# Turning the first two heads of a linear attention inside the last projection block, with gating, rounding and remainders in a new order

## The chip, the core and the metric

The kernel runs on one core of a Trainium2 chip. The metric is the device time of one execution in microseconds (us): 650.53 us, the median of three runs from 649.70 to 651.06. One more execution was profiled; it took 651.25 us, and its span, from the first to the last instruction, is 649.5 us.

## What is computed

A trunk of two residual layers over 256 tokens of width 1024. Layer 0 mixes tokens by gated linear attention (GLA), layer 1 by block softmax attention; a squared-ReLU MLP follows each. The change lies in the GLA mixer of layer 0:

```python
q, k, v, r, glr = jnp.split(h @ w_in, splits, axis=-1)
...
o = (o_intra + o_inter).reshape(B, S, H, DV)          # 4 heads of 256 columns
o = rms_norm(o, onorm_g).reshape(B, S, H * DV) * jax.nn.silu(r.astype(f32))
return o.astype(h.dtype) @ w_out
```

Each sub-layer is modulated with shift, scale and gate from `mod = silu(c) @ ada_w[i] + ada_b[i]`, a product over 6 x 1024 columns a layer.

## The kernel before, in words

The program is written out by hand for each engine. The order on an engine is the order of its instructions; engines meet at semaphores (`wait_ge`, `then_inc`).

Weights come from HBM through SyncE's queue (SP) into `w_raw`, 1 MB (two *units* of 128 x 1024) per copy, with four slots of 1 MB. ScalarE (ACT) rounds each unit to `w_hi` (`hi`, L1051), VectorE (DVE) makes the remainder `w_lo` (`lo`, L1433), and TensorE (PE) multiplies three times per product: hi by hi, lo by hi, hi by lo (`three`, L503 to L505). `w_hi` and `w_lo` hold four units each, so `hi(u)` waits until PE has used unit u-4. `lo(u)` of the second unit of a pair frees a slot of `w_raw`.

The GLA mixer has eight blocks of four units. Blocks 0 to 5 project k, q, v and r; (n, u) is unit u of block n. Blocks 6 and 7 are the output projection. PE accumulates a block of 0 to 5 in two PSUM banks: 4 and 5 for even n, 6 and 7 for odd n. ACT and DVE work one block ahead of PE's numbering: their step (6, u) rounds unit u of block 6 while PE is in block 5. Tables `tasks` say what else an engine does after each step.

Behind the recurrence, for two pairs of heads (0 and 1):

- ACT takes squares and roots (`o_squares`, `o_root`), DVE forms the scales (`o_scales`) and `normed(pair)`, two rows of heads per token tile out of PSUM (L1690, four instructions).
- ACT reads r's block out of PSUM through SiLU (`read_in(0, 4)`, `read_in(0, 5)`, L1163, two instructions each). It first loads the SiLU/sine table (`silu_set`, L1209); `sines` serves layer 1.
- DVE multiplies (`gated(pair)`, L1702, two instructions). It waits for `in_out`, ACT's reads, and for `on_ok`, its own `normed`.
- PE turns the result (`turn_o(pair)`, L660, eight 128 x 128 transposes) into banks 4 and 5 (pair 0) or 6 and 7 (pair 1). It waits for `ot_ok`, the gated pair.
- ACT rounds each turned head (`o_hi`, L1158) to `a_hi` and DVE makes `a_lo` (`o_low`, L1587). Head q is used by unit q of block 6, which waits for `a_ok`.

Before the change, PE runs `turn_o(0)` behind block 5, then two products `fin_gate` for the gates (L622), which wait for `on_ok` 2, then block 6, with `turn_o(1)` behind its first unit and `sum_mods(1, 4)` (L583) behind its fourth. DVE's loop ends with `lo(6, 3)`, then `o_low` of heads 0 and 1, `gated(1)`, two `gate` (L1486), `o_low` of heads 2 and 3, and two `ada()`. Block 7 follows, with `turn_mods` (L591) on PE and `mods` (L1472) on DVE, then the residual, its norm `xn` (L1509) and PE's turn of `xn` (L631), which opens the MLP.

The modulation product for later sub-layers is made by DVE in pieces. `ada()` number s (from 0) takes 1 MB of `ada_w` from one of two buffers `ada_raw` in two instructions (L1450; the first of a group of four is L1447) and counts `ada_mac` up by 2. The copies are issued by GpSimd (POOL, L381), in order:

```python
for s in range(2, 4 * N_PAIRS_ADA):
    pool.wait_ge(ada_mac, 2 * (s - 1))
    load(s)
```

So copy s starts once `ada()` s-2 is done. `sum_mods` begins with `pe.wait_ge(ada_mac, 8 * (ada_turn(b0 + 3) + 1))`; for `sum_mods(1, 4)` that is 24, which is the end of `ada()` number 11. Of the twelve, one stands ahead of the loop, eight at the steps listed in `adas`, one in the task (5, 3), and two behind the loop.

Of the kernel before, what the change touches and what calls it, by code (L numbers as in the profile page):

```python
# [29 lines left out]
ACT = mybir.ActivationFunctionType  # L30
# [3 lines left out]
TB = 2  # L34
COLS = 512
# [12 lines left out]
def trunk_kernel(nc, x_d, c_d, pos_d, ada_w, ada_b, mix_g, mlp_g, gla_in, gla_up, gla_bg, gla_og,  # L48
                 gla_out, moba_in, moba_qg, moba_kg, moba_out, w1_d, w2_d, eye_d, keep_d, amask_d,
                 restart_d, invf_d, out_d):  # L50
    DEPTH, D = mix_g.shape
# [29 lines left out]
    with ctx:  # L81
# [67 lines left out]
        silu_r = area(2 * K1, TB, D)  # L149
# [144 lines left out]
        def in_bank(n, tb):  # L294
            return 4 + 2 * (n % 2) + tb
# [203 lines left out]
        def _(pe):  # L499
# [153 lines left out]
            def turn_o(pair):  # L653

                pe.wait_ge(in_out, 10 + 2 * pair)
                pe.wait_ge(ot_ok, pair + 1)
                for h in (2 * pair, 2 * pair + 1):
                    for k in (2 * h, 2 * h + 1):
                        for tb in range(TB):
                            z = tr(ps[:, 4 + h, (k % 2) * SEQ + tb * P:(k % 2) * SEQ + (tb + 1) * P],  # L660
                                   o_tok[:, tb, k * P:(k + 1) * P], eye[:, :])
                    z.then_inc(oT_ok, 1)
# [106 lines left out]
            def gla():  # L769
# [86 lines left out]
                def first_blocks(sides):  # L856

                    for s, (n, u) in enumerate(FIRST):
# [13 lines left out]
                        if (s, 2) in sides:  # L872
# [3 lines left out]
                         {0: turn_k, 1: turn_q, 3: turn_tail},  # L876
                         {0: scores, 2: lambda: update(0), 3: lambda: update(1)},
                         {0: lambda: update(2), 1: lambda: update(3), 2: lambda: output(0), 3: lambda: output(1)},
                         {}]
                pe.wait_ge(mod_red, 2)  # L880
                first_blocks({(0, 2): lambda: second_rows(2), (1, 2): lambda: (second_cols(2), second_rows(3)),
                              (2, 0): lambda: second_cols(3), (5, 2): glr, (6, 2): logits})
                for n in range(2, 6):
                    pe.wait_ge(in_out, 2 * (n - 1))
                    project(mix_base[0] + 4 * n, (in_bank(n, 0), in_bank(n, 1)), None, sides[n])
                turn_o(0)
                pe.wait_ge(on_ok, 2)
                for i in range(2):
                    fin_gate(4 + i, 2 + i)
# [133 lines left out]
        def _(act):  # L1023
# [3 lines left out]
            def link(ins):  # L1027

                steps[0] += 1
                ins.then_inc(act_step, 1)  # L1030
                act.wait_ge(act_step, steps[0])
# [21 lines left out]
            def hi_at(u):  # L1053
                hi(u, u % 8, u // 8)
# [105 lines left out]
            def read_in(l, n, dst, func=ACT.Copy):  # L1160
                act.wait_ge(unit_used, FIRST_DONE[n] if l == 0 and n < 2 else mix_base[l] + 4 * n + 4)
                for tb in range(TB):
                    A(dst[tb], ps[:, in_bank(n, tb), :], func).then_inc(in_out, 1)  # L1163

            def gla():
                def glr():
                    act.wait_ge(glr_p, 1)
                    A(glrT[:, :], ps[:, 0, 0:SEQ], ACT.Copy).then_inc(glr_ok, 1)

                def softplus():  # L1170

                    act.wait_ge(z_p, 1)
                    for h in range(GH):
                        if h == 2:
                            act.wait_ge(z_ok, 2)
                        A(g_t[:, h], ps[:, h // 2, (h % 2) * SEQ:(h % 2 + 1) * SEQ], ACT.Abs,
                          bias=cols[:, C_BG + h:C_BG + h + 1]).then_inc(za_ok, 1)
                    act.wait_ge(za_ok, GH)
                    link(A(g_t, g_t, ACT.Exp, scale=-1.0))
                    A(g_t, g_t, ACT.Ln, bias=1.0).then_inc(ez_ok, 1)  # L1180

                def decays():
                    act.wait_ge(G_ok, 1)
                    A(g_i, g_s, ACT.Exp, scale=-1.0 / 16).then_inc(eG_ok, 1)
                    A(g_t, g_t, ACT.Exp, scale=1.0 / 16).then_inc(eG_ok, 1)
                    A(g_e, g_s, ACT.Exp, scale=1.0 / 16).then_inc(eG_ok, 1)

                def tail():
                    act.wait_ge(kt_p, 1)
                    for tb in range(TB):  # L1190
                        z = A(k_tail[:, tb], ps[:, 2 + tb, :].rearrange("p (h d) -> p h d", h=GH), ACT.Copy)
                    z.then_inc(kt_ok, 1)

                def o_squares(pair):
                    act.wait_ge(o_p, pair + 1)
                    for tb in range(TB):
                        for h in (2 * pair, 2 * pair + 1):
                            j = S_O + 4 * tb + h
                            A(o_tok[:, tb, h * DV:(h + 1) * DV],
                              ps[:, 2 * pair + tb, (h % 2) * DV:(h % 2 + 1) * DV],  # L1200
                              ACT.Square, accum_out=stat[:, j:j + 1]).then_inc(oss_ok, 1)

                def o_root():
                    act.wait_ge(oss_ok, 8)
                    link(A(stat[:, S_O + 8:S_O + 16], stat[:, S_O:S_O + 8], ACT.Ln, scale=1.0 / DV, bias=eps[:, :]))
                    A(stat[:, S_O + 16:S_O + 24], stat[:, S_O + 8:S_O + 16], ACT.Exp, scale=-0.5).then_inc(or0_ok, 1)

                def silu_set():
                    nc.scalar.preload_act_table_set(SETS_SILU_SIN)  # L1209

                def sines():
                    act.wait_ge(sc_arg, 1)
                    A(trig[:, :, :], trig[:, :, :], ACT.Sin).then_inc(sc_ok, 1)

                def ln_exp_set():
                    nc.scalar.preload_act_table_set(SETS_LN_EXP)

                def k_in():
                    glr()
                    read_in(0, 0, [g_tok[:, 0, tb] for tb in range(TB)])  # L1220


                tasks = {
                    (2, 0): [k_in],
                    (2, 2): [softplus],
                    (2, 3): [lambda: read_in(0, 1, [g_tok[:, 1, tb] for tb in range(TB)]), decays],
                    (3, 2): [tail],
                    (3, 3): [lambda: read_in(0, 2, [g_v[:, tb, 0:COLS] for tb in range(TB)])],
                    (4, 3): [lambda: read_in(0, 3, [g_v[:, tb, COLS:D] for tb in range(TB)])],
                    (5, 2): [lambda: o_squares(0)],  # L1230
                    (5, 3): [lambda: o_squares(1), o_root],
                    (6, 0): [silu_set, sines,
                             lambda: read_in(0, 4, [silu_r[:, tb, 0:COLS] for tb in range(TB)], ACT.Silu)],
                    (6, 2): [lambda: read_in(0, 5, [silu_r[:, tb, COLS:D] for tb in range(TB)], ACT.Silu)],
                }
                for n in range(2, 7):
                    for u in range(4):
                        hi_at(mix_base[0] + 4 * n + u)
                        for t in tasks.get((n, u), []):
                            t()  # L1240
                for q in range(4):
                    o_hi(0, q)
                ln_exp_set()

# [166 lines left out]
        def _(dve):  # L1411
# [178 lines left out]
            def o_low(l, qs=range(4)):  # L1590
                for q in qs:
                    a_low(A_OUT[l] + q, q, ps[:, 4 + q, :].rearrange("p (c t) -> p c t", c=2), slice(0, SEQ))
# [22 lines left out]
            def gla():  # L1615
# [69 lines left out]
                def normed(pair):  # L1685

                    r = stat[:, S_O + 40:S_O + 48]
                    for tb in range(TB):
                        for h in (2 * pair, 2 * pair + 1):
                            z = V.scalar_tensor_tensor(o_tok[:, tb, h * DV:(h + 1) * DV],  # L1690
                                                       ps[:, 2 * pair + tb, (h % 2) * DV:(h % 2 + 1) * DV],
                                                       r[:, 4 * tb + h:4 * tb + h + 1], onorm[:, :],
                                                       op0=ALU.mult, op1=ALU.mult)
                    z.then_inc(on_ok, 1)

                def gated(pair):

                    cs = slice(pair * COLS, (pair + 1) * COLS)
                    dve.wait_ge(in_out, 10 + 2 * pair)
                    dve.wait_ge(on_ok, pair + 1)  # L1700
                    for tb in range(TB):
                        z = V.tensor_tensor(o_tok[:, tb, cs], o_tok[:, tb, cs], silu_r[:, tb, cs], ALU.mult)  # L1702
                    z.then_inc(ot_ok, 1)
# [3 lines left out]
                    (3, 3): [masked], (4, 1): [lambda: states(0)], (4, 2): [lambda: states(1)],  # L1707
                    (5, 0): [lambda: states(2)], (5, 1): [lambda: states(3)],
                    (5, 3): [ada, o_scales, lambda: normed(0)],
                    (6, 0): [lambda: normed(1), lambda: gated(0)],  # L1710
                }

                ada()
                adas = [(2, 0), (3, 1), (3, 2), (4, 0), (4, 2), (5, 0), (5, 2), (6, 1)]
                for n in range(2, 7):
                    for u in range(4):
                        lo_at(mix_base[0] + 4 * n + u)
# [1 line left out]
                            t()  # L1719
                        if (n, u) in adas:  # L1720
                            ada()
                o_low(0, range(2))
                gated(1)
                for i in range(2):
                    gate(i, 2 + i)
                o_low(0, range(2, 4))
                for _ in range(2):
                    ada()

# [248 lines left out]
```

## Time and profile before

| | |
|---|---|
| median of three runs | 650.53 us (649.70 to 651.06) |
| profiled execution | 651.25 us, span 649.5 us, mean granted TensorE clock 0.983 |
| PE busy | 621.5 us, 96% of the span |
| DVE busy | 474.5 us, 73% |
| ACT busy | 341.0 us, 53% |
| the stretch of the change | about 114 to 154 us from the span's start |

All times below are counted from the span's start. A line of a timeline gives start, length, engine, line, operation, what is written from what, and how many merged instructions; the brackets give the engine's idle time before it and what ended it. The lengths of neighbouring instructions overlap (a matmul of 512 columns is listed with 0.39 us, but the next one starts 0.23 us later), so steps are counted from start to start.

### The profile page before, as it was taken

How to read it: one execution, taken by the hardware profiler on the slowest of the kernel's cores; microseconds unless marked ns; L12 is line 12 of the kernel's file. 1: busy time of each engine (PE TensorE's matmuls, PEld its weight loads, DVE VectorE, ACT ScalarE, POOL GpSimd, SP SyncE). 2: the span in 40 equal slices, each digit the busy share in tenths (PEclk: the TensorE clock that was granted, in tenths of full speed). 3: DMA queues.
4: the chain of work that ended last, by engine and by line, in shares of the span. 5: the costliest groups of instructions: out<-in, count | busy, mean ns of one | idle time of the engine just before them, and what ended most of it. 6: DMA issues, size and time to landing. Idle time of an engine off the chain costs nothing.

```text
span 649.5 us, 9093 instructions
## 1 busy us (share of the span) xinstructions
PE 621.5 (96%) x3391; PEld 516.6 (80%) x3391; DVE 474.5 (73%) x660; ACT 341.0 (53%) x581; POOL 39.4 (6%) x65
## 2 busy tenths in 40 slices
PE   4699999899999999999999989999999999999997
PEld 2467875677889988998977767788788899899885
DVE  4638998889768978888986777956886555555455
ACT  3437632658645344534458657666854543454440
POOL 3030021000000110111100000000000000000000
PEclk9599999999999999999999989999999999999999
DMA  8999499667588998999964644533476555555501
GB/s 287 387 359 391 164 329 381 219 250 257 190 279 322 373 364 306 360 347 355 364 240 160 208 152 147 178 112 121 157 245 225 186 187 193 194 194 194 192 1 65
DMA packets 59084, 156.43 MB, mean 241 GB/s; under 512 B 2818, under 2 KB 3312, under 8 KB 59056
## 3 DMA queue, kind: packets, MB, share of 16 engines
q1 hardware_dynamic: 47296, 112.41, 49.2%
q0 software_dynamic: 11760, 43.67, 18.9%
q8 instruction: 15, 0.25, 0.2%
q14 instruction: 13, 0.11, 0.0%
HBM read 155.02 MB, written 1.05 MB: 240 GB/s over the span
## 4 chain that ended last, share of the span: by engine, by line
PE 78%; DVE 12%; ACT 4%; issue 3%; DMA 2%; SPq 0%; DVEq 0%; ACTq 0%
PE ps L503 13%; PE ps L504 13%; PE ps L505 13%; PE ps L700 7%; PE ps L699 7%; PE ps L698 7%; PE ps L510 3%; PE ps L512 3%; PE ps L511 3%; DVE w_lo L1433 2%; DMA arena<-in_ada_w_dram 2%; DVE spare L1433 1%; PE ps L607 1%; DVE ada_acc L1450 1%; PE ps L615 1%
## 5 line engine op out<-in xcount | busy, mean ns | idle before, releaser
L1051 ACT ACTIVATE w_hi<-w_raw 128x1024 fp32r<-128x1024 f32 x180 | 189.1, 1058 | 215.4 <-PE ps L505 117.7
L1433 DVE TENSOR_TENSOR w_lo<-w_raw,w_hi 128x1024 fp32r<-128x1024 f32 x180 | 218.3, 1222 | 109.5 <-ACT w_hi L1051 109.3
L700 PE MATMUL ps<-a_hi,w_lo 128*128 128x256 f32 x384 | 108.7, 283 | 0.0
L699 PE MATMUL ps<-a_lo,w_hi 128*128 128x256 f32 x384 | 108.7, 283 | 0.0
L698 PE MATMUL ps<-a_hi,w_hi 128*128 128x256 f32 x384 | 108.6, 283 | 0.0
L503 PE MATMUL ps<-w_hi,m_hi 128*128 128x512 f32 x256 | 100.4, 392 | 0.0
L504 PE MATMUL ps<-w_lo,m_hi 128*128 128x512 f32 x256 | 99.8, 390 | 0.0
L505 PE MATMUL ps<-w_hi,m_lo 128*128 128x512 f32 x256 | 99.7, 389 | 0.0
L503 PE MATMUL ps<-w_hi,a_hi 128*128 128x512 f32 x224 | 93.0, 415 | 5.1 <-DVE a_lo L1587 5.1
L504 PE MATMUL ps<-w_lo,a_hi 128*128 128x512 f32 x224 | 88.6, 396 | 0.0
L505 PE MATMUL ps<-w_hi,a_lo 128*128 128x512 f32 x224 | 88.6, 396 | 0.0
L1450 DVE SCALAR_TENSOR_TENSOR ada_acc<-ada_raw,c_act,ada_acc 128x1024 f32<-128x1024 f32 x56 | 71.7, 1281 | 3.3 <-DMA ada_raw<-in_ada_w_dram 1.9
L699 PEld LDWEIGHTS ps<-a_lo,w_hi 128*128 128x128 f32 x384 | 73.7, 192 | 0.5
L698 PEld LDWEIGHTS ps<-a_hi,w_hi 128*128 128x128 f32 x384 | 73.7, 192 | 0.5
L700 PEld LDWEIGHTS ps<-a_hi,w_lo 128*128 128x128 f32 x384 | 73.7, 192 | 0.0
L503 PEld LDWEIGHTS ps<-w_hi,a_hi 128*128 128x128 f32 x224 | 42.9, 191 | 19.3 <-issue 7.4
L503 PEld LDWEIGHTS ps<-w_hi,m_hi 128*128 128x128 f32 x256 | 48.1, 188 | 11.1 <-DVE w_lo L1433 0.8
L505 PEld LDWEIGHTS ps<-w_hi,m_lo 128*128 128x128 f32 x256 | 48.1, 188 | 10.1
L504 PEld LDWEIGHTS ps<-w_lo,m_hi 128*128 128x128 f32 x256 | 48.1, 188 | 9.3
L381 POOL DMA_DIRECT2D ada_raw<-in_ada_w_dram x40 | 28.2, 704 | 412.7 <-DVE ada_acc L1450 368.7
L505 PEld LDWEIGHTS ps<-w_hi,a_lo 128*128 128x128 f32 x224 | 42.8, 191 | 9.4
L504 PEld LDWEIGHTS ps<-w_lo,a_hi 128*128 128x128 f32 x224 | 42.9, 191 | 8.1
(202 smaller groups left out, 712.6 us busy)
## 6 DMA issues: line engine op xcount, KB each, us to landing
w_raw<-in_mlp_w_dram SPq DMA_DIRECT2D x64, 1024.0 KB, 5.6
ada_raw<-in_ada_w_dram POOLq DMA_DIRECT2D x40, 1024.0 KB, 7.0
w_raw<-in_gla_w_in_dram SPq DMA_DIRECT2D x12, 1024.0 KB, 13.4
w_raw<-in_moba_w_in_dram SPq DMA_DIRECT2D x12, 1024.0 KB, 7.1
ada_raw<-in_ada_w_dram SPq DMA_DIRECT2D x4, 1024.0 KB, 13.0
arena<-in_ada_w_dram SPq DMA_DIRECT2D x4, 1024.0 KB, 14.2
w_raw<-in_gla_w_out_dram SPq DMA_DIRECT2D x4, 1024.0 KB, 9.0
w_raw<-in_moba_w_out_dram SPq DMA_DIRECT2D x4, 1024.0 KB, 4.8
```

The costliest lines, as they stand in the source:

```text
L381: nc.gpsimd.dma_start(ada_pair(s), src.rearrange("(k p) n -> p k n", p=P)).then_inc(ada_sw_in[s % 2], 16)
L503: mm(out, hi, w_hi[:, slot, wc], start=first, stop=False)
L504: mm(out, hi, w_lo[:, slot, wc], start=False, stop=False)
L505: return mm(out, lo, w_hi[:, slot, wc], start=False, stop=last)
L510: mm(out, hi, unit_hi(u)[:, wc], start=first, stop=False)
L511: mm(out, hi, unit_lo(u)[:, wc], start=False, stop=False)
L698: mm(o, w_hi[:, u, w], a_hi[:, a, :], start=u == 0 and k == 0, stop=False)
L699: mm(o, w_hi[:, u, w], a_lo[:, a, :], start=False, stop=False)
L700: z = mm(o, w_lo[:, u, w], a_hi[:, a, :], start=False, stop=u == 3 and k == 1)
L1051: A(dst, w_raw[:, c // 2, c % 2], ACT.Copy).then_inc(hi_made, 1)
L1433: V.tensor_tensor(out, w_raw[:, c // 2, c % 2], w.bitcast(F32), ALU.subtract).then_inc(lo_made, 1)
L1450: z = V.scalar_tensor_tensor(acc, w, c, acc, op0=ALU.mult, op1=ALU.add)
```

## The change

PE: `turn_o(0)` moves from behind block 5 to behind its third unit. ACT, step (6, 0): the SiLU read goes ahead of `sines`. Step (6, 2): `o_hi` of heads 0 and 1 goes ahead of the second SiLU read; only heads 2 and 3 stay behind the loop. DVE, step (6, 0): `gated(0)` goes ahead of `normed(1)`. Step (6, 1): `o_low` of heads 0 and 1 and `gated(1)` come in, `ada()` number 9 goes out. Step (6, 3): `ada()` number 9, then `o_low` of heads 2 and 3. The two `gate` and the last two `ada()` stay behind the loop.

```diff
-                         {}]
+                         {2: lambda: turn_o(0)}]
...
-                turn_o(0)
                 pe.wait_ge(on_ok, 2)
...
-                    (6, 0): [silu_set, sines,
-                             lambda: read_in(0, 4, [silu_r[:, tb, 0:COLS] for tb in range(TB)], ACT.Silu)],
-                    (6, 2): [lambda: read_in(0, 5, [silu_r[:, tb, COLS:D] for tb in range(TB)], ACT.Silu)],
+                    (6, 0): [silu_set,
+                             lambda: read_in(0, 4, [silu_r[:, tb, 0:COLS] for tb in range(TB)], ACT.Silu), sines],
+                    (6, 2): [lambda: o_hi(0, 0), lambda: o_hi(0, 1),
+                             lambda: read_in(0, 5, [silu_r[:, tb, COLS:D] for tb in range(TB)], ACT.Silu)],
...
-                for q in range(4):
+                for q in (2, 3):
                     o_hi(0, q)
...
-                    (6, 0): [lambda: normed(1), lambda: gated(0)],
+                    (6, 0): [lambda: gated(0), lambda: normed(1)],
+                    (6, 1): [lambda: o_low(0, range(2)), lambda: gated(1)],
+                    (6, 3): [ada, lambda: o_low(0, range(2, 4))],
...
-                adas = [(2, 0), (3, 1), (3, 2), (4, 0), (4, 2), (5, 0), (5, 2), (6, 1)]
+                adas = [(2, 0), (3, 1), (3, 2), (4, 0), (4, 2), (5, 0), (5, 2)]
...
-                o_low(0, range(2))
-                gated(1)
                 for i in range(2):
                     gate(i, 2 + i)
-                o_low(0, range(2, 4))
```

## Rows read from the trace of the kernel before

**Rows 1.** The page's chain that ended last: share of the span by engine.

```profile
PE 78%; DVE 12%; ACT 4%; issue 3%; DMA 2%; SPq 0%; DVEq 0%; ACTq 0%
```

**Rows 2.** Waits, 100 to 165 us: total, times, longest.

```profile
PE ps L503 <- DVE a_lo L1587: 1.8, 1, 1.8
```

**Rows 3.** Timeline of PE, blocks 5 and 6.

```profile
122.74 0.39 PE L503 MATMUL ps<-w_hi,a_hi 128*128 128x512 f32 x1
...
125.46 1.03 PE L660 MATMUL ps<-eye,arena 128*128 128x128 f32 x8
126.33 1.88 PE L622 MATMUL ps<-ada_acc,ones 128*128 128x512 f32 x4
129.98 0.47 PE L503 MATMUL ps<-w_hi,a_hi 128*128 128x512 f32 x1 [1.77 <-DVE a_lo L1587]
...
132.83 1.03 PE L660 MATMUL ps<-eye,arena 128*128 128x128 f32 x8
...
136.45 0.39 PE L503 MATMUL ps<-w_hi,a_hi 128*128 128x512 f32 x1
...
141.98 1.06 PE L583 MATMUL ps<-ada_acc,ones 128*32 128x512 f32 x8
```

**Rows 4.** Timeline of ACT, steps (6, 0) to (6, 3).

```profile
118.63 1.28 ACT L1209 ACT_TABLE_LOAD   x1
...
120.25 1.07 ACT L1163 ACTIVATE arena<-ps 128x512 f32<-128x512 f32 x2
...
123.00 1.06 ACT L1051 ACTIVATE w_hi<-w_raw 128x1024 fp32r<-128x1024 f32 x1 [0.73 <-PE ps L505]
125.66 1.09 ACT L1163 ACTIVATE arena<-ps 128x512 f32<-128x512 f32 x2 [1.60 <-PE ps L505]
...
127.58 1.09 ACT L1158 ACTIVATE a_hi<-ps 128x512 fp32r<-128x512 f32 x2
```

**Rows 5.** Timeline of DVE from step (6, 0) to the modulation of the MLP.

```profile
120.46 1.65 DVE L1690 SCALAR_TENSOR_TENSOR arena<-ps,stat,onorm 128x256 f32<-128x256 f32 x4
122.03 1.28 DVE L1702 TENSOR_TENSOR arena<-arena 128x512 f32<-128x512 f32 x2
...
124.36 2.60 DVE L1450 SCALAR_TENSOR_TENSOR ada_acc<-ada_raw,c_act,ada_acc 128x1024 f32<-128x1024 f32 x2
...
129.15 1.28 DVE L1587 TENSOR_TENSOR a_lo<-ps,a_hi 128x512 fp32r<-128x512 f32 x2
...
131.55 1.28 DVE L1486 TENSOR_TENSOR gates<-ps,gates 128x512 f32<-128x512 f32 x2
...
135.30 5.30 DVE L1450 SCALAR_TENSOR_TENSOR ada_acc<-ada_raw,c_act,ada_acc 128x1024 f32<-128x1024 f32 x4
140.52 4.63 DVE L1433 TENSOR_TENSOR w_lo<-w_raw,w_hi 128x1024 fp32r<-128x1024 f32 x4
146.48 0.17 DVE L1472 TENSOR_TENSOR modc<-ps,cols 128x16 f32<-128x16 f32 x1 [1.33 <-PE ps L591]
```

**Rows 6.** Timeline of PE at the turn of `xn`.

```profile
153.53 1.07 PE L631 MATMUL ps<-eye,arena 128*128 128x128 f32 x8 [0.27 <-DVE arena L1509]
```

**Rows 7.** Timeline of POOL: the issue of copy 11.

```profile
127.26 0.70 POOL L381 DMA_DIRECT2D ada_raw<-in_ada_w_dram  x1 [12.05 <-DVE ada_acc L1450]
```

**Rows 8.** L381, issues at 127 to 128, 138 to 139, 170 to 260 us.

```profile
DMA to landing us min/median/max: 5.5/5.5/5.5
...
DMA to landing us min/median/max: 5.8/5.8/5.8
...
DMA to landing us min/median/max: 5.4/6.8/8.9
```

**Rows 9.** Timeline of PE at its longest wait for DVE after 100 us.

```profile
375.99 1.97 PE L906 MATMUL ps<-eye,arena 128*128 128x128 f32 x8 [3.33 <-DVE arena L1764]
```

**Rows 10.** Windows: length, five engines' busy time, granted clock, DMA share, GB/s.

```profile
128.00:129.00 1.00, 0.21 (x1) 0.00 (x0) 1.00 (x2) 0.66 (x2) 0.00 (x0) 1.00 1.17 389
...
376.00:377.00 1.00, 1.00 (x5) 1.00 (x6) 1.00 (x2) 0.08 (x1) 0.00 (x0) 0.50 0.00 0
```

## The prediction, made before the changed kernel ran

> **What bounds the kernel now.** I read the chain that ended last first: 78% of it is PE, 12% DVE, 4% ACT [rows 1]. Time can be won only where PE stands still or where a hand-over from DVE or ACT paces it. Next the waits of the stretch of the change: PE waits once for a remainder, 1.8 us [rows 2]. Then the timelines of the single engines, in which the reader is to see how that gap is made. PE turns pair 0 at 125.46, starts the gate products at 126.33 and the first unit of block 6 only at 129.98, after 1.77 us of idleness ended by `a_lo` [rows 3]. ACT rounds the turned heads from 127.58 because `hi(6, 3)` and the SiLU read stand ahead of it [rows 4]; DVE makes `a_lo` from 129.15, behind `ada()` number 9 (124.36, 2.60 us) and two `lo` [rows 5]. Last I read what waits behind block 6: `sum_mods` starts at 141.98, as soon as block 6 is through, and it may, since `ada()` number 11 ended at 135.30 + 5.30 = 140.60 [rows 3, 5]. Its cover is 1.4 us. That is the point where I expect the gain to be handed back.
>
> **PE up to block 6.** The third unit of block 5 ends where the fourth starts, at 122.74; a unit takes 125.46 - 122.74 = 2.72 us [rows 3]. The turn now comes there. Its cost between two units, with the slower first matmuls behind it, is seen at `turn_o(1)`: from 132.83 to 136.45 are 3.62 us for a turn and a unit, so 0.90 for the turn [rows 3]. Behind block 5 it took 126.33 - 125.46 = 0.87. I take 0.90. The fourth unit then ends at 122.74 + 0.90 + 2.72 = 126.36, and the gate products start there, as before (126.33).
>
> Does the turn wait? ACT's table load ends at 119.91, and now the SiLU read follows it: 119.93 + 1.07 = 121.00 [rows 4]. `gated(0)` starts about 121.05 and ends at 122.33 (1.28 us) [rows 5]; PE asks at 122.74. Cover 0.4 us; if it were gone, PE would wait by the same amount and ACT too, since `hi(6, 3)` comes behind `o_hi`. `sines` behind the read costs nothing: ACT next waits for PE anyway, 0.73 us ahead of 123.00 [rows 4].
>
> ACT: `hi(6, 2)` runs from 123.00 to 124.06, then `o_hi` of two heads, 1.09 us, to 125.1 [rows 4]. DVE: `normed(1)` 1.65 us to 123.9, `lo(6, 1)` to 125.05 (a `lo` in a row takes (4.63 - 1.22) / 3 = 1.14 us from start to start, and 1.22 alone), `o_low` of two heads 1.28 us to 126.3 [rows 5]. The gate products end at 126.36 + 1.88 = 128.2 [rows 3] and everything that unit 0 of block 6 waits for is there. **The 1.77 us go entirely.** Block 6 starts at 128.21. With `turn_o(1)` behind its first unit it ends at 141.98 - 1.77 = 140.2, if it doesn't wait inside.
>
> **DVE and ACT behind that.** ACT's second SiLU read started 0.20 us after the turn of before, at 125.66 [rows 3, 4]; now it starts at 126.56 and ends at 127.65. `gated(1)` is 127.7 to 128.95. All `lo` behind it are pushed back, which is the wait that the change adds: `lo(6, 2)` to 130.1, `lo(6, 3)` to 131.2. PE wants unit 2 of block 6 at 128.21 + (136.45 - 129.98) = 134.7 [rows 3], so these are covered by over 3 us. `ada()` number 9 comes now, from 131.14 to 133.74, instead of from 124.36. `o_low` of heads 2 and 3 ends at 134.35 and 134.95; the first is asked for at 134.7. Cover 0.3 us, and if it is gone it costs nothing yet, as the next step shows. The gates end at 136.15 (1.28 us), `ada()` number 10 at 138.66 [rows 5].
>
> **The copy that comes too late.** The move of `ada()` number 9 by 131.14 - 124.36 = 6.8 us isn't only a move on DVE. It frees the buffer for copy 11, which POOL issues 0.30 us after its end (126.96 to 127.26) [rows 5, 7], so now at 134.04. No other copy is queued on POOL between. `ada()` number 11 can't start before it has landed. Bounds: the quickest of thirteen later copies took 5.4 us, the slowest 8.9 [rows 8]. The copy of before took 5.5 with weights in flight beside it, one issued into idle engines 5.8 [rows 8]. Here the weight copy released by `lo(6, 3)` at 131.2 is ahead by 2.8 us, so it is nearest to these two: I take 5.7. It lands at 139.74; with 0.05 for the semaphore and 2.60 for the piece, `ada()` number 11 ends at 142.39. Before it was 140.60.
>
> The Trainium skill, page "DMA: Bandwidth & Descriptors", section "Anatomy of one DMA — SWDGE (gpsimd) path", gives about 2.0 us plus the bytes over 436 GB/s for such a copy, so an estimate of 4.4 us for 1 MB. By it the piece would end at 141.1 and the kernel would be 0.6 us faster than before. No copy of the rows is that quick [rows 8], so I go by the rows and keep the rule as a small rival.
>
> PE therefore waits in `sum_mods` from 140.2 to 142.39 + 0.14 (129.15 plus one `a_lo`, 0.69 us, to 129.98 is such a hand-over) = 142.53, against 141.98 before: +0.55. Block 7's first unit needs its `lo`, which stands behind the piece: 142.31 + 1.22 + 0.14 = 143.67, while PE is free of `sum_mods` at 142.53 + 1.00 = 143.53. Another 0.14. Together **+0.7 us**; in general it is the end of `ada()` number 11 less 141.7.
>
> From here it travels undiminished: `mods` on DVE waited for PE's turn [rows 5], and its remaining `lo` end 4.55 us after the piece, no later than that turn; the residual, `xn` and PE's turn of `xn` follow without slack, as PE waited there for DVE [rows 6]. Later copies keep their distance to these steps, so I count nothing for them.
>
> The sum against the profiled execution: span 649.5 + 0.7 = 650.2, its time 651.25 + 0.7 = 651.95. That execution lies 0.7 above the median of 650.53, so the median of the changed kernel is forecast at **651.2 us**.
>
> **The rivals.** First, the whole gain stays: the stall of 1.77 us goes and `sum_mods` is not held. Then 650.53 - 1.77 = 648.8. For it speaks that the stall is real and that its cause is removed. Against it: `ada()` number 11 would have to end by 140.1, the copy to land in 3.4 us, or the order of copies to be other than I read it.
>
> Second, slower: the clock falls in the new wait. PE would idle some 2.3 us ahead of `sum_mods`. An idle time of 1.77 us left the granted clock at 1.00, that is 2.4 GHz; one of 3.33 us was followed by 0.50, that is 1.2 GHz [rows 3, 9, 10]. Mine lies between, nearer to the first. Eight transposes took 1.97 us there, against 1.03 [rows 3, 9]: 0.94 for the first microsecond of work. `sum_mods` would likewise pay 1.0, and the unit behind it some 0.5: +0.7 + 1.5 = +2.2, so 652.7. It decides from an idle time somewhere between 1.8 and 3.3 us.
>
> Third, also slower: copy 11 meets others and takes 8.9 us. 134.04 + 8.9 + 0.05 + 2.60 - 141.7 = +3.9, so 654.4. Against it: the engines are idle from about 135 on, as the next weight copy waits for `lo` of block 7.
>
> Fourth, nothing comes of it: the +0.7 is absorbed by slack I don't see, or by another phase of the copies: 650.5. The quick copy of the rule above gives 649.9.
>
> **How the numbers follow.** Forecast, with the copy at 5.4 to 6.4 us, +0.4 to +1.4: 0.60. Absorbed: 0.10. Quick copy: 0.05. Whole gain: 0.07. Clock: 0.10. Late copy: 0.08. A measurement of this kernel tells about 0.2%, 1.3 us, from no change. Faster by more is the whole gain and a little of the quick copy, 0.09; slower by more is the clock, the late copy and the upper end of the forecast, 0.21; the rest, 0.70, lies within. The range from 650.0 to 652.7 leaves out the whole gain, the late copy and some of the clock's case, about 0.2 together.
>
> **What the profile after would show.** PE: the turn (L660) between third and fourth unit of block 5 without a wait, and no idle time at the first unit of block 6. ACT and DVE: `a_hi` and `a_lo` of pair 0 done before the gate products end. POOL: copy 11 issued near 134 instead of 127. DVE: a wait for `ada_raw` from a copy, about 1.1 us, ahead of the piece that ends at 142.4. PE: an idle time of about 2.3 us ahead of L583, which then starts near 142.5, with the granted clock at 1.00. The forecast is wrong if L583 starts before 141 (then the gain stays), if the clock falls there, or if `xn` is turned at the same time as before in spite of a late L583.

## The result, and the profile after

| | before | changed |
|---|---|---|
| median | 650.14 us (648.27 to 652.02, 20 runs) | 652.0 us (649.72 to 655.51, 20 runs) |
| ratio | 1 | 1.0031, 95% interval 1.0019 to 1.0043 |
| profiled execution | 651.25 us, span 649.5 | 653.92 us, span 652.1 |

The changed kernel is slower by 0.31%, 2.0 us, where the forecast had 0.7. The forecast was 651.2 us, the range 650.0 to 652.7.

The two profiled executions already differ by 0.5 us ahead of the change, so I measure from the end of the third unit of block 5 to PE's turn of `xn`: before 122.74 to 153.53, 30.79 us [rows 3, 6]. PE after the change (start, length, engine, line, operation, count, idle time ahead with its releaser):

```profile
123.26 1.03 PE L660 MATMUL ps<-eye,arena 128*128 128x128 f32 x8
...
126.89 1.88 PE L622 MATMUL ps<-ada_acc,ones 128*128 128x512 f32 x4
...
131.38 1.03 PE L660 MATMUL ps<-eye,arena 128*128 128x128 f32 x8
...
142.72 1.07 PE L583 MATMUL ps<-ada_acc,ones 128*32 128x512 f32 x8 [2.00 <-DVE ada_acc L1450]
143.94 0.55 PE L503 MATMUL ps<-w_hi,a_hi 128*128 128x512 f32 x1 [0.16 <-DVE w_lo L1433]
144.28 0.63 PE L504 MATMUL ps<-w_lo,a_hi 128*128 128x512 f32 x1
144.71 0.63 PE L505 MATMUL ps<-w_hi,a_lo 128*128 128x512 f32 x1
...
148.35 0.60 PE L591 MATMUL ps<-eye,arena 128*128 128x128 f32 x4
...
156.04 1.07 PE L631 MATMUL ps<-eye,arena 128*128 128x128 f32 x8 [0.26 <-DVE arena L1509]
```

The turn stands between the third and the fourth unit, without a wait. The stall of 1.77 us behind the gate products is gone. A new one of 2.00 us stands ahead of L583. From 123.26 to 156.04 are 32.78 us, 1.99 more than before. Of these only 0.22 are there when L583 starts (142.72 - 123.26 = 19.46, against 141.98 - 122.74 = 19.24). The other 1.77 lie between L583 and L591: 5.63 us against 3.86. The line of L591 before:

```profile
145.84 0.60 PE L591 MATMUL ps<-eye,arena 128*128 128x128 f32 x4
```

DVE and POOL show why L583 waits:

```profile
125.48 1.28 DVE L1587 TENSOR_TENSOR a_lo<-ps,a_hi 128x512 fp32r<-128x512 f32 x2
128.20 1.29 DVE L1702 TENSOR_TENSOR arena<-arena 128x512 f32<-128x512 f32 x2 [1.44 <-ACT arena L1162]
...
131.69 2.60 DVE L1450 SCALAR_TENSOR_TENSOR ada_acc<-ada_raw,c_act,ada_acc 128x1024 f32<-128x1024 f32 x2
...
140.06 2.60 DVE L1450 SCALAR_TENSOR_TENSOR ada_acc<-ada_raw,c_act,ada_acc 128x1024 f32<-128x1024 f32 x2 [0.87 <-DMA ada_raw<-in_ada_w_dram]
```

```profile
134.57 0.70 POOL L381 DMA_DIRECT2D ada_raw<-in_ada_w_dram  x1 [18.84 <-DVE ada_acc L1450]
```

`ada()` number 9 now starts at 131.69, copy 11 is issued at 134.57 (before: 124.36 and 127.26 [rows 5, 7]) and lands 5.5 us later; DVE waits 0.87 us for it, and number 11 ends at 142.66. DVE also stands idle for 1.44 us ahead of `gated(1)`, which waits for ACT's second SiLU read; the piece that filled this time before now stands behind it. And this is what lies behind L583, in windows of 1 us (length, busy time and count of PE, weight loads, DVE, ACT, POOL, then PE's granted clock, DMA share, GB/s):

```profile
141.00:142.00 1.00, 0.00 (x0) 0.00 (x0) 0.96 (x2) 0.81 (x1) 0.00 (x0) 1.00 0.74 164
142.00:143.00 1.00, 0.28 (x4) 0.16 (x8) 1.00 (x2) 0.00 (x0) 0.04 (x1) 1.00 0.92 352
143.00:144.00 1.00, 0.84 (x9) 0.09 (x1) 1.00 (x2) 0.15 (x1) 0.66 (x1) 1.00 0.99 410
144.00:145.00 1.00, 1.00 (x3) 0.83 (x4) 1.00 (x2) 1.00 (x2) 0.00 (x0) 0.60 0.59 180
145.00:146.00 1.00, 1.00 (x4) 0.72 (x4) 1.00 (x2) 1.00 (x2) 0.00 (x0) 0.50 0.86 213
146.00:147.00 1.00, 1.00 (x4) 0.81 (x3) 1.00 (x2) 1.00 (x2) 0.00 (x0) 0.50 0.91 360
147.00:148.00 1.00, 1.00 (x5) 0.81 (x4) 0.20 (x1) 1.00 (x2) 0.00 (x0) 0.69 1.05 389
```

The clock falls to 1.2 GHz near 144.2, after PE has resumed, and is back at 2.4 GHz near 147.6. PE is busy all that time, which is why a row of busy shares shows nothing; the matmuls start 0.43 us apart instead of 0.23 and are listed with 0.63 us instead of 0.39. Before, this stretch had a clock of 1.00 throughout:

```profile
144.00:145.00 1.00, 1.00 (x6) 0.82 (x5) 1.00 (x2) 1.00 (x2) 0.00 (x0) 1.00 1.04 418
145.00:146.00 1.00, 1.00 (x7) 0.79 (x6) 0.15 (x1) 1.00 (x2) 0.00 (x0) 1.00 0.87 309
```

### The profile page after: what moved, and what is told of

It is laid out like the page before. It is cut to its first block, busy times and chain, and to the rows that moved or that the text cites. A ratio compares the mean times of both kernels' runs of the same rounds, so it can differ in the third digit from the quotient of the medians.

```text
span 652.1 us, 9093 instructions
## 1 busy us (share of the span) xinstructions
PE 623.8 (96%) x3391; PEld 517.5 (79%) x3391; DVE 474.5 (73%) x660; ACT 341.0 (52%) x581; POOL 39.4 (6%) x65
## 4 chain that ended last, share of the span: by engine, by line
PE 78%; DVE 12%; ACT 4%; DMA 3%; issue 3%; SPq 0%; DVEq 0%; ACTq 0%
PE ps L503 13%; PE ps L505 13%; PE ps L504 13%; PE ps L700 7%; PE ps L699 7%; PE ps L698 7%; PE ps L510 3%; PE ps L512 3%; PE ps L511 3%; DVE w_lo L1433 2%; DMA arena<-in_ada_w_dram 2%; DVE ada_acc L1450 1%; PE ps L607 1%; DVE spare L1433 1%; DMA ada_raw<-in_ada_w_dram 1%
## 5 line engine op out<-in xcount | busy, mean ns | idle before, releaser
L503 PE MATMUL ps<-w_hi,a_hi 128*128 128x512 f32 x224 | 94.4, 422 | 3.5 <-DVE a_lo L1587 3.3
L505 PE MATMUL ps<-w_hi,a_lo 128*128 128x512 f32 x224 | 90.0, 402 | 0.0
L1450 DVE SCALAR_TENSOR_TENSOR ada_acc<-ada_raw,c_act,ada_acc 128x1024 f32<-128x1024 f32 x56 | 71.7, 1280 | 2.2 <-DMA ada_raw<-in_ada_w_dram 0.9
L381 POOL DMA_DIRECT2D ada_raw<-in_ada_w_dram x40 | 28.2, 704 | 414.9 <-DVE ada_acc L1450 368.1
```

The source lines that it names most:

```text
L381: nc.gpsimd.dma_start(ada_pair(s), src.rearrange("(k p) n -> p k n", p=P)).then_inc(ada_sw_in[s % 2], 16)
L503: mm(out, hi, w_hi[:, slot, wc], start=first, stop=False)
L505: return mm(out, lo, w_hi[:, slot, wc], start=False, stop=last)
L1450: z = V.scalar_tensor_tensor(acc, w, c, acc, op0=ALU.mult, op1=ALU.add)
```

## The experiments

Ratios are to the kernel before, run on the same chip beside them, each from 6 to 20 runs of the kernel. "Stretch" is the time from the end of block 5's third unit to the turn of `xn` in the profile: 30.79 us before. The third unit ends where the turn L660 starts, or, where the turn stands behind block 5, where the fourth unit starts, 2.72 us ahead of L660. The stretch, the idle time and the clock are those of one profiled execution per row. Lines that a kernel adds or drops shift the numbers of those behind them: the piece is L1450 or, with such a shift, L1451, L1456 or L1459.

| kernel | ratio, 95% interval | stretch, against before | idle ahead of L583 | clock behind it |
|---|---|---|---|---|
| changed | 1.0031 (1.0019 to 1.0043) | 32.78, +1.99 | 2.00 | falls |
| changed, again | 1.0052 (1.0033 to 1.0070) | 32.80, +2.01 | 2.09 | falls |
| piece early | 0.9956 (0.9935 to 0.9976) | 28.93, -1.86 | none | 1.00 |
| piece early, again | 0.9951 (0.9938 to 0.9963) | 28.87, -1.92 | none | 1.00 |
| own buffer | 0.9983 (0.9965 to 1.0000) | 30.45, -0.34 | 1.20 | 1.00 |
| PE busy | 1.0004 (0.9988 to 1.0019) | 31.52, +0.73 | 0.26 | 1.00 |
| turn back | 1.0034 (1.0018 to 1.0049) | 33.15, +2.36 | 2.08 | falls |
| turn back, piece first | 0.9974 (0.9958 to 0.9991) | 29.18, -1.61 | none | 1.00 |
| late piece alone | 1.0032 (1.0014 to 1.0051) | 32.66, +1.87 | 1.89 | 1.00 |

**Piece early.** `ada()` number 9 leaves step (6, 3) for step (6, 1).

```diff
-                    (6, 1): [lambda: o_low(0, range(2)), lambda: gated(1)],
-                    (6, 3): [ada, lambda: o_low(0, range(2, 4))],
+                    (6, 1): [lambda: o_low(0, (0,)), ada, lambda: o_low(0, (1,)), lambda: gated(1)],
+                    (6, 3): [lambda: o_low(0, range(2, 4))],
```

> The changed kernel, but ada() number 9 stands in step (6, 1) between o_low of head 0 and of head 1 instead of in step (6, 3). Theory (the gain is handed back because copy 11 is issued 6.8 us late, and then the clock falls in the wait for the piece that uses it): ada() 9 ends near 128.6, POOL issues copy 11 near 129 and it lands near 134.5, ahead of its use; DVE is then busy without a break and ends ada() 11 near 140.3. L583 starts near 140.5 after at most 0.5 us of idle time, the granted clock stays 1.00, and the kernel is 1.4 us faster than before (ratio 0.998). Rival (the loss comes from the new order on PE and ACT, not from the piece): it stays 2 us slower than before.

PE and POOL of this kernel:

```profile
120.06 1.03 PE L660 MATMUL ps<-eye,arena 128*128 128x128 f32 x8
123.69 1.88 PE L622 MATMUL ps<-ada_acc,ones 128*128 128x512 f32 x4
128.17 1.03 PE L660 MATMUL ps<-eye,arena 128*128 128x128 f32 x8
137.33 1.07 PE L583 MATMUL ps<-ada_acc,ones 128*32 128x512 f32 x8
```

```profile
125.78 0.70 POOL L381 DMA_DIRECT2D ada_raw<-in_ada_w_dram  x1 [13.24 <-DVE ada_acc L1450]
```

No idle time up to L583; copy 11 is issued 5.7 us behind the third unit, against 11.3 in the changed kernel. One instruction pair turns +2 us into a gain, 1.86 us in the stretch where 1.4 was expected. DVE does the piece (2.6 us) from 122.89, and `gated(1)` starts only 1.0 us later for it (5.94 us behind the third unit against 4.94), since the piece fills the 1.44 us in which DVE stood idle. The rival falls: PE and ACT have the same order in both. L583 starts 137.33 - 120.06 = 17.27 us behind the third unit, 1.97 earlier than before.

**Own buffer.** The order of the change, but copy 11 has a buffer of its own.

```diff
-                nc.gpsimd.dma_start(ada_pair(s), src.rearrange("(k p) n -> p k n", p=P)
-                                    ).then_inc(ada_sw_in[s % 2], 16)
+                dst, done = (own, own_in) if s == 11 else (ada_pair(s), ada_sw_in[s % 2])
+                nc.gpsimd.dma_start(dst, src.rearrange("(k p) n -> p k n", p=P)
+                                    ).then_inc(done, 16)
...
-                pool.wait_ge(ada_mac, 2 * (s - 1))
+                if s == 11:
+                    pool.wait_ge(o_p, 2)
+                else:
+                    pool.wait_ge(ada_mac, 2 * (s - 1))
```

> The changed kernel with its order kept, but copy 11 goes to 1 MB of its own (free since the outputs of the attention), so POOL issues it right behind copy 10, near 116, and it waits for no piece. Theory: DVE's 0.9 us wait for the copy goes, ada() 11 ends near 141.2 instead of 142.3, PE idles about 1.0 us ahead of L583 instead of 2.0, the clock stays at 1.00 and the kernel is about 0.4 us faster than before (ratio 0.999), 2.4 us better than the change. If DVE's order alone and not the copy made the wait: L583 as late as in the changed kernel and 2 us slower than before.

DVE ahead of `gated(1)` (here L1711), `ada()` number 11 (L1459, out of `arena`, the buffer of its own) and L583 (here L589); the third unit ends at 119.91:

```profile
124.85 1.29 DVE L1711 TENSOR_TENSOR arena<-arena 128x512 f32<-128x512 f32 x2 [1.43 <-ACT arena L1168]
...
135.94 2.60 DVE L1459 SCALAR_TENSOR_TENSOR ada_acc<-arena,c_act,ada_acc 128x1024 f32<-128x1024 f32 x2
138.60 1.07 PE L589 MATMUL ps<-ada_acc,ones 128*32 128x512 f32 x8 [1.20 <-DVE ada_acc L1459]
```

The copy's own part is thus 0.8 us of L583's delay: its wait of 0.87 us goes, the idle time falls from 2.00 to 1.20, and the clock stays. The 1.20 us that are left are DVE's order: it still stands idle for 1.43 us ahead of `gated(1)`, with number 9 behind it.

**PE busy.** Nine matmuls without use ahead of the wait.

```diff
+                    def busy():
+                        pe.wait_ge(gate_ok, 2)
+                        for i in range(9):
+                            mm(ps[:, 2, :], a_hi[:, i % 4, 0:P], a_hi[:, 4:6, :].rearrange("p a n -> p (a n)"),
+                               start=True, stop=True)
...
-                    out_project({0: lambda: turn_o(1), 3: lambda: sum_mods(1, 4)},
+                    out_project({0: lambda: turn_o(1), 3: lambda: (busy(), sum_mods(1, 4))},
```

> The changed kernel with nine 512-column matmuls (2.0 us, into PSUM bank 2, which block 7 overwrites) ahead of PE's wait in sum_mods(1, 4). Nothing else moves: L583 starts as late as in the changed kernel. Theory (the clock falls because PE idles 2.0 us): the granted clock stays 1.00 through block 7, its first matmuls keep 0.23 us from start to start instead of 0.43, and the kernel is 0.5 us slower than before (ratio 1.0008), 1.5 us better than the change. Rival (block 7's first units are slowed by something else, such as the copies and weights landing then): 2 us slower than before, as the change.

```profile
140.77 1.06 PE L583 MATMUL ps<-ada_acc,ones 128*32 128x512 f32 x8 [0.26 <-DVE ada_acc L1456]
142.00 0.47 PE L503 MATMUL ps<-w_hi,a_hi 128*128 128x512 f32 x1 [0.16 <-DVE w_lo L1439]
144.85 0.60 PE L591 MATMUL ps<-eye,arena 128*128 128x128 f32 x4
```

```profile
143.00:144.00 1.00, 1.00 (x6) 0.82 (x5) 1.00 (x1) 1.00 (x2) 0.00 (x0) 1.00 0.87 233
144.00:145.00 1.00, 1.00 (x7) 0.78 (x6) 1.00 (x2) 1.00 (x2) 0.00 (x0) 1.00 0.94 385
```

L583 is no earlier than in the changed kernel (19.75 us behind the third unit, against 19.46, since copy 11 took 0.3 us longer), yet L591 follows it after 4.08 us instead of 5.63. Work of no use makes the kernel faster than the change, by 1.26 us in the stretch; the ratio falls from 1.0031 to 1.0004, with intervals that only touch. The price of the clock, 1.55 us, is shown by itself, and copies in flight beside block 7 cost nothing that is seen.

**Turn back.** PE's part undone: `turn_o(0)` stands behind block 5 again.

```diff
-                         {2: lambda: turn_o(0)}]
+                         {}]
...
+                turn_o(0)
                 pe.wait_ge(on_ok, 2)
```

> The changed kernel with turn_o(0) back behind block 5, so the orders on ACT and DVE alone. Theory (what removed the stall of 1.77 us is that o_hi and o_low of heads 0 and 1 no longer stand behind other work; the gate products, 1.9 us, cover them): no idle time at block 6 even so; gated(1) and all behind it on DVE end 0.4 us later, so L583 starts 0.4 us later than in the changed kernel and the kernel is 2.4 us slower than before (ratio 1.0037). Rival (PE's early turn is what removes the stall): 1.8 us of idle time at block 6 come back, the idle time ahead of L583 shrinks by as much, the clock stays 1.00 and the kernel is 0.6 to 1.0 us slower than before.

```profile
124.38 1.03 PE L660 MATMUL ps<-eye,arena 128*128 128x128 f32 x8
125.25 1.88 PE L622 MATMUL ps<-ada_acc,ones 128*128 128x512 f32 x4
129.72 1.03 PE L660 MATMUL ps<-eye,arena 128*128 128x128 f32 x8
133.94 0.47 PE L503 MATMUL ps<-w_hi,a_hi 128*128 128x512 f32 x1 [0.44 <-DVE a_lo L1588]
141.70 1.36 PE L583 MATMUL ps<-ada_acc,ones 128*32 128x512 f32 x8 [2.08 <-DVE ada_acc L1451]
```

The stall at block 6 is gone here too. The words of the change name PE's turn; what removes the stall is that ACT and DVE round heads 0 and 1 ahead of other work, covered by the gate products. L583 starts 20.04 us behind the third unit, 0.58 later than in the changed kernel, where 0.4 was expected. One thing was late: the third unit of block 6 waits 0.44 us for `o_low` of head 2. In the changed kernel that unit starts at 135.03, 0.15 us behind the end of head 2's `a_lo` (134.20 + 0.68), so the cover of 0.3 us was all but used up there too.

**Turn back, piece first.** The same, with `ada()` number 9 first in step (6, 1).

```diff
-                    (6, 1): [lambda: o_low(0, range(2)), lambda: gated(1)],
-                    (6, 3): [ada, lambda: o_low(0, range(2, 4))],
+                    (6, 1): [ada, lambda: o_low(0, range(2)), lambda: gated(1)],
+                    (6, 3): [lambda: o_low(0, range(2, 4))],
```

> The changed kernel with turn_o(0) back behind block 5, and with ada() number 9 first in step (6, 1), ahead of o_low of heads 0 and 1, instead of in step (6, 3). DVE then does the piece while PE is still in block 5, and waits for no turn. Theory (the early turn on PE brings nothing of its own; the gate products cover the rounding of heads 0 and 1, and only the piece's place matters): at most 0.3 us of idle time at block 6, copy 11 issued about 2 us after the third unit's end plus 3 (near 128 on the clock of before), L583 without a wait above 0.4 us, clock 1.00, and 1.4 to 1.8 us faster than before (ratio 0.9975), the same as with the early turn and the piece between the two remainders. Rival (the early turn is needed): 1.0 us or more of idle time at block 6 and no gain over before.

No idle time at block 6 or ahead of L583. The early turn isn't needed for the gain. Whether it adds something can't be told: the stretch is 0.25 us longer than with the early turn (and the piece stands one step earlier), and the intervals of the ratios overlap.

The profiled execution was the slowest of this kernel's twelve, 651.06 us against a median of 647.47. It shows the same chain once more, in a part of the program that nobody changed:

```profile
307.68 2.60 DVE L1451 SCALAR_TENSOR_TENSOR arena<-ada_raw,c_act,arena 128x1024 f32<-128x1024 f32 x2 [4.68 <-DMA ada_raw<-in_ada_w_dram]
313.88 0.50 PE L503 MATMUL ps<-w_hi,m_hi 128*128 128x512 f32 x1 [2.13 <-DVE m_lo L1834]
```

The copy took 10.2 us instead of the 5.7 of before, and PE idled 2.13 us. The clock fell at 314.5, after PE had resumed, for 3.4 us. No other profile has that idle time. The idle time and the slow clock make up most of the 4.1 us by which the rest of this execution, from the turn of `xn` on, is longer than before (649.3 - 149.25 = 500.05 us against 495.97).

**The change again.** The changed kernel, unaltered.

> The changed kernel once more, beside the others. Theory: 2 us slower than before (ratio 1.003), from the end of the third unit of block 5 to the turn of xn 32.8 us in a profile with the clock's fall, against 30.8 before. If the fall of the clock hangs on how the wait lies to something that isn't in the program, single runs differ in their mean granted clock by about 0.003 (3 us at half clock are 0.0024 of the span).

```profile
142.65 1.07 PE L583 MATMUL ps<-ada_acc,ones 128*32 128x512 f32 x8 [2.09 <-DVE ada_acc L1450]
```

The profile repeats the first: 2.09 us idle, then 0.50 for 3.4 us, and a stretch 2.01 us longer than before. The ratio, 1.0052, came out higher than the 1.003 expected; its interval overlaps that of the first 20 runs, and no profile shows what the part above 2 us would be. Single runs of the changed kernel differ in their mean clock: in 13 of the first 20 it was 0.984 or less, in seven 0.986 or more. A fall of 3.4 us at half clock is 0.0026 of the span. That fits a fall that comes in most runs and not in all. But here it was 0.984 or less in only 5 of 11 runs, and in the kernel before in 8 of 30 and 3 of 28, so the share isn't shown.

**Late piece alone.** The kernel before, with nothing but `ada()` number 9 moved behind the gates.

```diff
-                adas = [(2, 0), (3, 1), (3, 2), (4, 0), (4, 2), (5, 0), (5, 2), (6, 1)]
+                adas = [(2, 0), (3, 1), (3, 2), (4, 0), (4, 2), (5, 0), (5, 2)]
...
                     gate(i, 2 + i)
+                ada()
                 o_low(0, range(2, 4))
```

> The kernel before with one part of the change alone: ada() number 9 leaves step (6, 1) and stands behind the two gates, 8 us later; everything else as before. Theory: the stall of 1.8 us at block 6 stays (a little shorter, 1.5), copy 11 is issued near 135 and lands near 141, ada() 11 ends near 143.5, PE idles about 1.9 us ahead of L583, the clock falls behind it, and the kernel is 3.3 us slower than before (ratio 1.005); without the clock's fall 1.8 us slower (ratio 1.0028). Rival (the late piece is harmless and the loss belongs to the new order on PE and ACT): no difference from before.

```profile
124.18 1.03 PE L660 MATMUL ps<-eye,arena 128*128 128x128 f32 x8
125.05 1.88 PE L622 MATMUL ps<-ada_acc,ones 128*128 128x512 f32 x4
128.41 0.47 PE L503 MATMUL ps<-w_hi,a_hi 128*128 128x512 f32 x1 [1.48 <-DVE a_lo L1587]
131.25 1.03 PE L660 MATMUL ps<-eye,arena 128*128 128x128 f32 x8
142.37 1.06 PE L583 MATMUL ps<-ada_acc,ones 128*32 128x512 f32 x8 [1.89 <-DVE ada_acc L1450]
```

DVE ahead of the `a_lo` that ends PE's wait of 1.48 us:

```profile
126.44 1.23 DVE L1433 TENSOR_TENSOR w_lo<-w_raw,w_hi 128x1024 fp32r<-128x1024 f32 x1 [2.14 <-ACT w_hi L1051]
```

Moving one piece of modulation costs 2 us by itself, as the working without the clock's fall said (1.8, ratio 1.0028). The fall that I expected didn't come in this profile. The kernel also shows whose order made the stall of before: with the piece out of the way 1.48 of the 1.77 us stay, as DVE then waits 2.14 us for `hi(6, 3)`, which stands behind the SiLU read on ACT and ahead of `o_hi`.

**Piece early, again.** The same kernel as in the first experiment.

> The kernel with the early turn and ada() number 9 between o_low of head 0 and head 1, once more, since its first measurement (ratio 0.9956, interval 0.9935 to 0.9976, seven runs) lay lower than its profile explains: from the end of block 5's third unit to the turn of xn it is 1.9 us shorter than before. Theory: the true ratio is that of 1.6 to 1.9 us, 0.9971 to 0.9975, the same as with the turn behind block 5. If the early turn brings something that the profile's stretch doesn't show, the ratio stays at 0.9956, 2.8 us.

The stretch is 28.87 us (121.44 to 150.31), 1.92 shorter than before, but the ratio stays at 0.9951, 3.2 us. This version beats both kernels: median 646.79 us beside 650.36. The part above 1.9 us shows in one more place. All the kernels wait 3.3 us at the first turn of rotated keys (L905, L906 or L911). In eight profiles the clock fell there; in the two of this kernel it didn't. PE and the windows of the second:

```profile
372.57 1.09 PE L905 MATMUL ps<-eye,arena 128*128 128x128 f32 x8 [3.32 <-DVE arena L1763]
...
384.85 1.09 PE L905 MATMUL ps<-eye,arena 128*128 128x128 f32 x8 [0.26 <-DVE arena L1763]
```

```profile
371.00:372.00 1.00, 0.00 (x0) 0.00 (x0) 0.93 (x3) 0.94 (x5) 0.00 (x0) 1.00 0.01 4
372.00:373.00 1.00, 0.43 (x4) 0.43 (x5) 1.00 (x2) 0.66 (x1) 0.00 (x0) 1.00 0.00 0
373.00:374.00 1.00, 1.00 (x10) 0.92 (x8) 1.00 (x2) 0.30 (x1) 0.00 (x0) 1.00 0.00 0
```

From this turn to the next of the same line are 12.28 us here; before they were 13.60, from 375.99 [rows 9] to this line:

```profile
389.59 1.10 PE L906 MATMUL ps<-eye,arena 128*128 128x128 f32 x8 [0.27 <-DVE arena L1764]
```

The other seven profiles have 13.75 to 14.84 there. That accounts for the missing 1.3 us in the profiles. Why it doesn't fall here isn't settled: two profiles may be luck.

## Why the prediction came out as it did

The time lies in the range, and the direction was right, but the case that came wasn't the one I called likeliest. It was the second rival, "the clock falls in the new wait", with 652.7 us and a chance of 0.10; the forecast of 651.2 lies 0.8 us below the measured median. Between the two kernels the runs show 2.0 us where the forecast had 0.7; part of that is hidden in the absolute time, since 20 runs put the kernel before at 650.14 and not at 650.53. The time is in the range because the range was drawn out to the clock's case, not because the likeliest case was right. The sentence on what the range leaves out also forgets the quick copy, 649.9, with its 0.05.

- **The stall of 1.77 us goes entirely, and the turn doesn't wait.** Right. The gate products start 3.63 us behind the turn's start; I had 3.62.
- **The copy that comes too late.** Right, to a tenth: I had copy 11 issued 11.30 us behind the third unit, and it was 134.57 - 123.26 = 11.31. Piece early, own buffer and late piece alone show it from three sides.
- **+0.55 at L583.** Too much: 0.22. The copy took 5.5 us instead of 5.7, the piece followed its landing at once, and PE the piece after 0.06 us where I had put 0.14. The Trainium skill's rule for such a copy, page "DMA: Bandwidth & Descriptors", section "Anatomy of one DMA — SWDGE (gpsimd) path", an estimate of 4.4 us, was met by no copy of this stretch: the three took 5.5, 5.4 and 5.9 us.
- **+0.14 for block 7's `lo`.** Right: 0.16.
- **"Mine lies between, nearer to the first"** is the step that failed. I weighed the fall of the clock by the length of the idle time alone, between 1.77 us (no fall) and 3.33 us (fall), and gave it 0.10. It cost 5.63 - 3.86 - 0.16 = 1.61 us in the profile and 1.55 by the experiment with PE kept busy. My price of 1.5 was right as a sum and wrong in its place, which is luck in part: in the row that it was taken from the clock fell at 375.4, while PE still waited, so the first work behind the wait was slow. Here `sum_mods` ran at full clock, and the fall came 1.5 us into the work behind the wait.
- **It travels undiminished.** Right: +1.99 at the turn of `xn`, and from there to the end of the span 495.97 us before and 496.06 after.

## What to carry to other kernels

Before a piece of work is moved back on an engine, look for what its end releases on a queue with few buffers: here 2.6 us of VectorE work, moved 6.8 us, delayed a copy and through it opened a wait on TensorE behind block 6. When a change fills one idle time on TensorE and opens another, price the second with a possible fall of the clock and give that real weight: here the new idle time, net of the old one, cost 0.2 us and the slow matmuls behind it 1.6. And undo the parts one by one: the move on TensorE that gave the change its name wasn't needed to remove the stall; the new order on ScalarE and VectorE did that alone.

## What the runs showed of the hardware

The length of an idle time on TensorE didn't decide by itself whether the clock fell. Idle times of 1.20, 1.48, 1.77 and 1.89 us were followed by none; 2.00, 2.08, 2.09 and 2.13 us, each seen once, by a fall to 1.2 GHz; 3.3 us by one in eight profiles and by none in two. In the three falls at block 7 and the one at 314.5 us the engine was already at work again, for 0.6 to 1.5 us, when its clock went down, and the clock was back after 3.4 us. Of the eight falls at the first turn of rotated keys three came while PE still waited and five 0.5 to 1.4 us after it had resumed. In the kernel with PE kept busy the clock stayed down there for 6.8 us; from that turn to the next are 14.84 us instead of 13.60, which makes that kernel's rest 1.1 us longer than before (649.6 - 152.54 = 497.06 us against 495.97) though nothing there was changed.

The opening of the kernel, up to the third unit of block 5, took between 119.9 and 123.3 us in the ten profiles, with the same program on PE there. A single execution says nothing on a difference of 2 us; the stretch around the change does.
